# Down projection of the feed-forward taken token chunk by token chunk, with the mixer norm's steps placed inside the last pair

## What is computed

```python
s1, sc1, g1, s2, sc2, g2, s3, sc3, g3 = ada(c, w_ada, b_ada)      # silu(c) @ w_ada + b_ada
h = x + 0.5 * g1 * swiglu(modulate(x, g_ffn1, s1, sc1), w1_gate, w1_up, w1_down)
n = modulate(h, g_mix, s2, sc2)          # rmsnorm(h) * g * (1 + scale) + shift
z = n @ w_in                             # 5192 columns: indexer k, indexer q, q, k, v, conv GLU, gates
...
h = h + g2 * mix
h = h + 0.5 * g3 * swiglu(modulate(h, g_ffn2, s3, sc3), w2_gate, w2_up, w2_down)
```

## Time and profile before

| what | value |
|---|---|
| time, median of 3 runs | 3036.06 us (3033.57 to 3036.47) |
| span of the profiled execution, first to last instruction | 3039.2 us |
| PE busy | 2838.8 us, 93% of the span |
| DVE busy | 1560.0 us, 51% |
| ACT busy | 579.2 us, 19% |
| POOL busy | 748.4 us, 25% |
| mean granted clock of PE | 0.952 |

### The profile page before, as it was taken

The page is one execution under the profiler, slowest core; times in us unless marked ns, Lnnn a source line. Parts: engine busy times, 40 slices in busy tenths (PEclk is TensorE's granted clock), DMA queues, the critical chain, the costliest instruction groups (busy, mean ns, idle before and its releaser), DMA issues.

```text
span 3039.2 us, 43529 instructions
## 1 busy us (share of the span) xinstructions
PE 2838.8 (93%) x16084; PEld 2516.0 (83%) x16084; DVE 1560.0 (51%) x2609; ACT 579.2 (19%) x1056; POOL 748.4 (25%) x419
## 2 busy tenths in 40 slices
PE   7999999999998899999994999888889999999996
PEld 3799999999996667888992356588889999999995
DVE  2443433333347379999998348763243333333335
ACT  1411111111113221122112234420040001010113
POOL 0322222222221236323320000022212332232320
PEclk9999999999999999999996769999989999999998
DMA  6322222222222323211226100123101111111101
GB/s 229 118 70 69 69 69 69 69 69 69 69 66 91 97 57 86 85 35 49 93 81 232 32 1 1 43 87 132 42 22 49 48 41 48 41 48 48 48 21 57
DMA packets 207445, 209.09 MB, mean 69 GB/s; under 512 B 13071, under 2 KB 160643, under 8 KB 206457
## 3 DMA queue, kind: packets, MB, share of 16 engines
q1 hardware_dynamic: 197180, 181.04, 18.9%
q10 hardware_dynamic: 10181, 26.90, 2.7%
HBM read 172.37 MB, written 28.94 MB: 66 GB/s over the span
## 4 chain that ended last, share of the span: by engine, by line
PE 72%; DVE 17%; issue 4%; ACT 3%; DMA 2%; DVEq 1%; SPq 1%; ACTq 0%; POOL 0%; POOLq 0%
PE main L244 19%; PE main L245 18%; PE main L246 18%; DVE top L1129 6%; DVE pick L1142 5%; PE main L1442 3%; PE aux L1469 3%; PE main L1458 2%; PE aux L414 2%; PE main L333 1%; DVE pick L1116 1%; ACT tmp L454 1%; PE aux L344 1%; PE aux L343 1%; PE aux L342 1%
## 5 line engine op out<-in xcount | busy, mean ns | idle before, releaser
L244 PE MATMUL main<-nhi,whi 128*128 128x352 f32 (+1 forms) x3288 | 1076.2, 327 | 29.6 <-DVE nlo L505 18.2
L246 PE MATMUL main<-nhi,wlo 128*128 128x352 f32 (+1 forms) x3288 | 1063.3, 323 | 0.0
L245 PE MATMUL main<-nlo,whi 128*128 128x352 f32 (+1 forms) x3288 | 1062.9, 323 | 0.0
L233 POOL CAST whi<-raw 128x1024 fp32r<-128x1024 f32 x189 | 200.0, 1058 | 2144.3 <-PE main L246 1722.5
L244 PEld LDWEIGHTS main<-nhi,whi 128*128 128x128 f32 (+1 forms) x3288 | 622.5, 189 | 56.4 <-issue 22.8
L245 PEld LDWEIGHTS main<-nlo,whi 128*128 128x128 f32 (+1 forms) x3288 | 624.1, 190 | 0.8
L246 PEld LDWEIGHTS main<-nhi,wlo 128*128 128x128 f32 (+1 forms) x3288 | 622.3, 189 | 0.7
L235 POOL TENSOR_TENSOR wlo<-raw,whi 128x1024 fp32r<-128x1024 f32 x189 | 475.5, 2516 | 15.2
L638 DVE TENSOR_TENSOR tmp<-main,tmp 128x352 f32<-128x352 f32 x132 | 69.2, 524 | 780.0 <-PE main L246 776.1
L659 DVE SCALAR_TENSOR_TENSOR h<-main,ada,h 128x352 f32<-128x352 f32 (+1 forms) x528 | 294.3, 567 | 94.9 <-PE main L246 94.8
L244 PE MATMUL main<-hid_hi,whi 128*128 128x352 f32 x1056 | 341.7, 324 | 0.3
(11 more groups left out here) (224 smaller groups left out, 2570.5 us busy)
## 6 DMA issues: line engine op xcount, KB each, us to landing
ada_raw<-in_w_ada SPq DMA_DIRECT2D x18, 2048.0 KB, 8.7
raw<-in_w_gate SPq DMA_DIRECT2D x44, 512.0 KB, 3.9
raw<-in_w_up SPq DMA_DIRECT2D x44, 512.0 KB, 3.8
raw<-in_w_down SPq DMA_DIRECT2D x44, 512.0 KB, 3.4
raw<-in_w_in SPq DMA_DIRECT2D x40, 512.0 KB, 3.9
gate_d<-zraw ACTq DMA_DIRECT2D x16, 528.0 KB, 2.7
gates<-gate_d SPq DMA_DIRECT2D x16, 528.0 KB, 4.9
zsw<-zraw ACTq DMA_DIRECT2D x50, 132.0 KB, 2.4
```

Source lines behind the costliest of these rows:

```text
L233: pool.tensor_copy(whi[:, slot], raw[:, slot]).then_inc(hi_done, 1)
L244: pe.matmul(bank, whi[:, slot, w], hi(c), start=(i == 0), stop=False)
L245: pe.matmul(bank, whi[:, slot, w], lo(c), start=False, stop=False)
L246: last = pe.matmul(bank, wlo[:, slot, w], hi(c), start=False, stop=(i == n - 1))
```

## The change

1. In every pair of both feed-forwards the down products go chunk by chunk: d = 8 t + 4 half + m. `pe_ada_split` moves from between d = 11 and 12 to ahead of t = 1, between d = 7 and 8. `FFN_ENDS` has 32 in place of 24, since half 0 is now used until d = 19.
2. The last pair of the first feed-forward is taken out of the loops and written out. The mixer norm is a new function, `norm_late`, whose steps stand among those of that pair: squares of chunk 0 on ACT behind d = 7, its sums on PE ahead of d = 12, its reciprocal and scaling on DVE ahead of d = 12 and d = 16, the sums of chunk 1 on PE ahead of d = 20. All squares are made by ACT, into the part of `nlo` that chunk 2 will take (`sq_late`).
3. The remaining steps of the norm are put in another order, and the waits for all 24 updates are gone from PE, ACT and DVE; z's first products wait for their banks instead. `small` gets a place of its own.

```diff
-FFN_ENDS = (5, 6, 9, 12, 24, 36)
+FFN_ENDS = (5, 6, 9, 12, 32, 36)
...
+        sq_late = place("sq_late", [P, KD, TOK], F32, NB + KD * TOK * 4)
...
+            sql = sq_late[:, :, 2 * TC:TOK]
...
+            def square(act, t):
+                done(act, t)
+                if t:
+                    norm_wait(act, q, "mm", t)
+                for half in range(2):
+                    c4 = slice(4 * half, 4 * half + 4)
+                    act.activation(sql[:, c4, :], h[:, c4, tcs(t)], ACT.Square).then_inc(s["sq"], 1)
...
+            def act(act, between):
+                square(act, 0)
+                between()
+                act.wait_ge(mod_set, 4)
+                root(act, 0)
+                square(act, 1)
+                affine(act, 0, (0,))
+                root(act, 1)
+                affine(act, 0, (1,))
+                square(act, 2)
+                affine(act, 1, (0,))
+                root(act, 2)
+                affine(act, 1, (1,))
+                affine(act, 2)
...
+            def rest(dve):
+                low(dve, 0, (0,))
+                rstd_of(dve, 1)
+                low(dve, 0, (1,))
+                done(dve, 1)
+                scale(dve, 1)
+                low(dve, 1, (0,))
+                rstd_of(dve, 2)
+                low(dve, 1, (1,))
+                done(dve, 2)
+                scale(dve, 2)
+                norm_wait(dve, q, "mm", 3)
+                low(dve, 2)
...
-                for half in range(2):
-                    if with_ada and half:
+                for t in range(NTC):
+                    if with_ada and t == 1:
                         if first:
                             pe.wait_ge(c_split, 2)
                         pe_ada_split(pe, INIT_ADA // 4 + j, aux[:, 0])
-                    pe.wait_ge(split_done, T0 + 6 * j + 4 + half + 1)
-                    for t in range(NTC):
+                    for half in range(2):
+                        if t == 0:
+                            pe.wait_ge(split_done, T0 + 6 * j + 4 + half + 1)
                         if half == 0:
                             ffn_wait(pe, q, "hid_lo", 6 * j + 3 + t + 1)
+                        if last and t and half:
+                            if t == 1:
+                                pe_ada_turn(pe, INIT_ADA // 4 + j, aux[:, 1], ada_rows[1])
+                            else:
+                                pe.wait_ge(ada_out, INIT_ADA // 4 + j + 2)
+                            then["pe_sums"](pe, (t - 1,))
                         for m in range(4):
-                            d = 12 * half + 4 * t + m
+                            d = 8 * t + 4 * half + m
...
-                        half, t, m = d // 12, d % 12 // 4, d % 4
-                        c = 4 * half + m
+                        t, c = d // 8, d % 8
+                        if last and d == 12:
+                            dve_ada(dve, INIT_ADA // 4 + j, aux[:, 1])
+                            then["dve_rstd"](dve, 0)
+                        if last and d == 16:
+                            then["dve_scale"](dve, 0)
...
+                if then:
+                    act_step(act, NPAIR - 1)
+                    then["act"](act, lambda: act_ada(act, INIT_ADA // 4 + NPAIR - 1, aux[:, 0], ada_rows[1]))
...
+                if then:
+                    dve_mod(dve, 1, ROW_GM, INIT_ADA // 4 + NPAIR - 1)
+                    dve_mod(dve, 2, ROW_G2, INIT_ADA // 4 + NPAIR - 1)
+                    dve_step(dve, NPAIR - 1, last=True)
+                    dve_half_gate(dve, 2)
+                    then["dve_rest"](dve)
...
         def m1_pe(pe):
-            ffn_wait(pe, "1", "down_free", 24 * NPAIR + 24)
-            norm_m["pe_start"](pe)
             for t in range(NTC):
                 for L in range(2):
                     norm_m["ready"](pe, t)
                     z_product(pe, L, T_Z + L, L % RING, 3 * L, L % 2, 72 if L == 0 else P, ts=(t,))
                     if L == 0 and t == 0:
-                        norm_m["pe_last"](pe)
+                        norm_m["pe_sums"](pe, (2,))
```

More of the change, by code:

```diff
@@ L524, in ffn @@
+        def ffn(q, T0, A0, wg, wu, wd, i, nrm, with_ada, then=None):
+            NLOOP = NPAIR - 1 if then else NPAIR
             f = ffn_sem
@@ L564, in pe_up, with pe_step @@
                         lambda c: nhi[:, c, tcs(t)], lambda c: nlo[:, c, tcs(t)], 0).then_inc(acc_done, 1)
-            def pe_step(pe, j, first):
+            def pe_step(pe, j, first, last=False):
                 for t in range(NTC):
@@ L596, in pe_step @@
                                     m * P, mstride=512).then_inc(acc_done, 1)
-                if with_ada:
+                if with_ada and not last:
                     pe_ada_turn(pe, INIT_ADA // 4 + j, aux[:, 1], ada_rows[1])
@@ L602, in pe @@
                 pe_step(pe, 0, True)
-                with pe.Fori(1, NPAIR) as j:
+                with pe.Fori(1, NLOOP) as j:
                     pe_step(pe, j, False)
+                if then:
+                    pe_step(pe, NPAIR - 1, False, last=True)
             def up_done(j, sub, t, up):
@@ L615, in dve_free, with act_step, chunk_done, dve_step @@
                 dve.drain().then_inc(f["down_free"], 24)
+            def act_step(act, j):
+                for sub in range(2):
+                    for t in range(NTC):
+                        act.wait_ge(acc_done, up_done(j, sub, t, 0))
+                        act.activation(tmp[:, t, :], main[:, t, 0:TC], ACT.Silu).then_inc(f["gate_free"], 1)
+                        ffn_wait(act, q, "up_free", 3 + 6 * j + 3 * sub + t + 1)
+                        act.activation(hid_hi[:, sub, tcs(t)], tmp[:, 3 + t, :], ACT.Copy).then_inc(f["hid_hi"], 1)
+                if with_ada:
+                    for i in range(4):
+                        act_ada_hi(act, INIT_ADA // 4 + j, i)
             def act(act):
                 norm_wait(act, q, "lo", 6)
[L619 to L626, removed]
+                with act.Fori(0, NLOOP) as j:
+                    act_step(act, j)
                     if with_ada:
-                        for i in range(4):
-                            act_ada_hi(act, INIT_ADA // 4 + j, i)
                         act_ada(act, INIT_ADA // 4 + j, aux[:, 0], ada_rows[1])
-            def dve(dve):
-                with dve.Fori(0, NPAIR) as j:
+                if then:
+                    act_step(act, NPAIR - 1)
+                    then["act"](act, lambda: act_ada(act, INIT_ADA // 4 + NPAIR - 1, aux[:, 0], ada_rows[1]))
+            def chunk_done(eng, t):
+                ffn_wait(eng, q, "down_free", 24 * NPAIR + 8 * t + 8)
+            def dve_step(dve, j, last=False):
                     for sub in range(2):
@@ L656, in dve @@
                                               ALU.mult).then_inc(f["samp"], 1)
-                            ffn_wait(dve, q, "samp", 8 * j + 4 * half + m + 1)
+                            ffn_wait(dve, q, "samp", 8 * j + c + 1)
                             dve.tensor_tensor(h[:, c, SEQ:TOK], h[:, c, SEQ:TOK], small[:, c, :], ALU.add)
@@ L661, in dve @@
                             .then_inc(f["down_free"], 1)
-                    if with_ada:
+                    if with_ada and not last:
                         dve_ada(dve, INIT_ADA // 4 + j, aux[:, 1])
+            def dve(dve):
+                with dve.Fori(0, NLOOP) as j:
+                    dve_step(dve, j)
+                if then:
+                    dve_mod(dve, 1, ROW_GM, INIT_ADA // 4 + NPAIR - 1)
[3 more added lines that the diff above has]
+                    then["dve_rest"](dve)
             return {"sp": sp, "pool": pool, "pe": pe, "act": act, "dve": dve, "act_free": act_free,
-                    "dve_free": dve_free}
+                    "dve_free": dve_free, "chunk_done": chunk_done}
         w_in = L0["w_in"]
@@ L854, in z_product @@
             for t in ts:
+                if L < 2:
+                    ffn_wait(pe, "1", "down_free", 24 * NPAIR + 19 + 3 * parity + t)
                 pe.wait_ge(z_free, V + t + 1)
@@ L1921, in _ @@
             act.drain().then_inc(ada_copy, 1)
+            act.drain().then_inc(z_free, 6)
             act_init(act)
```

74 lines of the change are left out of this document (60 added, 14 removed).

## The result

| | changed kernel | kernel before, same chip |
|---|---|---|
| median of 4 runs | 3062.27 us (3059.16 to 3067.95) | 3036.26 us (3033.57 to 3040.64) |
| span of the profiled execution | 3057.2 us | 3039.2 us |

The ratio is 1.0091, with a 95% interval from 1.0072 to 1.0109: the change costs 26.0 us by the medians. The forecast was 3068, with a range from 3049 to 3080.

A forecast was written before the change was run, and what follows sets the result against it. The prediction took PE to bound the feed-forward pairs. Stall +24.2, clock +15 and norm -7 summed to +32 us on a median of 3036.1, giving 3068 us, with a range of 3049 to 3080.

The forecast's parts named there:

- Bound by PE in the pairs: Feed-forward pairs: PE sets the pace, so the change can gain or lose only PE's idle time and clock.
- Stall 11 x 2.2 = +24.2: Conditioning in eleven pairs: PE waits about 2.5 us for `ada_lo` where it waited 0.3, +24.2 us.
- Clock 8 x 1.9 = +15: Behind the conditioning's stall: PE's clock falls in eight of eleven pairs, 1.9 us each, +15 us, bounds 0 and +21.
- The norm -7: Mixer norm in the last pair: chunk 2's z product at about 987 us, before 994.32; -7 us, range -10 to -2.
- clock stays full: Rival, behind the stalls in the pairs: no clock is lost, +15 us in all, 3051 us; chance 0.17.
- Chunk order nothing: Down products in the pairs: apart from the conditioning, the new chunk order costs nothing, 0 us.
- the walk of the last pair: Last pair of the first feed-forward: step-by-step timing of the norm to chunk 2's z product, about 987 us.
- Rotary table 0, bound 2: SP behind the norm: the rotary table goes no sooner than 1004.1 us; cost put at 0, other bound 2 us.
- The sum: Whole kernel: 24.2 + 15 - 7 = +32 us on the median of 3036.1, giving 3068 us.
- What would show it: Profile signs: about 2.5 us idle before L343 in eleven pairs, low PE clock digits from 100 to 950 us, slow conditioning matmuls, late rotary table.

The follow-up runs named there:

- filled kernel: The changed kernel with twelve matmuls of no use ahead of the wait for `ada_lo` in each of eleven pairs; 3050.06 us, ratio 1.0042.
- d = 11 kernel: The changed kernel with the conditioning products moved from ahead of d = 8 to ahead of d = 11; 3025.68 us, ratio 0.996.

## Why the prediction was right, point by point

- **Bound by PE in the pairs: right.** All 32 us of the first ten pairs are PE's own idle time and clock, and filling the idle time alone gave back the clock.
- **Stall 11 x 2.2 = +24.2: right in size**, though one of the eleven stands in the norm's term too (below). There were eleven waits of 2.4 to 2.5 us where 0.3 was. The term was sound because `ada_lo`'s completion could be read as a time after d = 0 (10.1, then 10.2), and nothing upstream of it moved.
- **Clock 8 x 1.9 = +15: right that it is lost, lucky in the count, too high in the price.** Eight pairs lost it, at 1.5 us each, +12. Nothing in the rows gave eight rather than five or eleven, and the kernel with the conditioning moved alone, with the same waits, lost it in five. The 1.9 came from a stretch of other matmuls (fp32 sums), and was a little high even for those: the sums at full clock began at 100.49 and not at 100.65, which makes it 1.8; the conditioning's take 0.63 in place of 0.40, and 3.4 us of them lose 1.5. The rival "clock stays full" was wrong, and the rule beside it lets too much pass: the Trainium skill (TensorE: Matmul & The Clock Gate, Why this matters for your kernels) warns only of idle gaps longer than these, while here 2.4 us of idle time lost the clock in eight pairs of eleven. With the clock full, the change would have come out at about 3050 (3062.27 - 12; the filled kernel measured 3050.06).
- **Chunk order nothing: right**, shown by itself at 1.000.
- **The norm -7: the mechanism right, the sum not.** The step at fault is in the sum: the walk of the last pair already held that pair's stall, and then eleven stalls were added, so that 2.2 us stand twice. By the walk's own measure, last d = 0 to chunk 2's z product, 77.4 us were foreseen and 80.9 came. Of the 3.5 more, 1.5 is the clock of the eleventh conditioning, priced in the other term, so -5.3 stands against -7.3. Another 1.2 came up to the last update, 0.75 of it one L788 held beside POOL's cast (0.94 us in place of 0.19), and 1.7 between that and the first z product, where L390 stood; behind it the steps were 0.9 shorter, although the first z product was slower (6.25 for 5.5). Two guesses inside it came out well: the sums of chunk 1 waited 1.38 (1.4 foreseen), and the table load stood behind the wait for the sums.
- **Rotary table 0, bound 2: 0.9** in the changed kernel, inside the bound. The same idle time was longer by 1.9 in the d = 11 kernel and by 3.6 in the filled one, so the bound was too tight for those.
- **The sum.** +32 was foreseen. By the measured terms, ten stalls of 2.2 outside the last pair, 12 of clock and -5.3, it is 22 + 12 - 5.3 = +28.7; the two profiles show +28.5 up to chunk 2's first z product, and the medians +26.0. The price of the clock and the stall counted twice made the sum too high by 3 and 2.2, the norm's steps ran 2 us longer than in the walk, and so part of the error cancelled. The forecast of 3068 stands 5.7 us above the result.
- **What would show it.** The wait at L343 and the long matmuls were there; the low digits of the clock were not, since a digit is an average over 76 us.

## What to carry to other kernels

Before a step is moved to an earlier place in an engine's program, read for each thing it waits for how long after a common event it is ready, and compare that with the new arrival: here 10.1 us against 7.6, eleven times over, and one call placed three products later turned +26 us into -9. A short wait in front of TensorE can cost more than its length (2.4 us of wait cost 3.9 in eight pairs here), so look for low clock behind it in the timeline, not in the coarse row, and put useful work (here the sums) into the idle time instead of behind it. When one collision between DVE and POOL is taken away, see which DVE step takes its place before counting the gain.

## What was not expected of the hardware

- **Half clock behind 2.4 us of idle time, in some pairs only.** Equal waits of 2.4 to 2.5 us behind some 75 us of full work each lost the clock in 8 of 11 pairs here, and in 5 of 11 in the kernel with the conditioning moved alone. A wait of 1.5 us lost it in none of 11. What decides between equal waits is left open here.
- **A small DVE step held for the whole of a POOL step.** L390, on 72 elements a partition, took 2.06 us beside POOL's subtraction (985.43, 2.35 us long) and 0.19 where POOL was idle; with it moved away, `nlo` took 3.48 there in place of 1.6. The Trainium skill (SBUF — State Buffer, Who interferes with whom) says that a `tensor_scalar` in its two-port form and a `tensor_tensor` with both inputs in SBUF contend with a GpSimd instruction that reads SBUF for a shared pair of ports, which is locked, so that the one that comes second has to stand; the two traces agree, with those numbers. In the changed kernel's timeline, POOL's row:

```profile
985.43 2.35 POOL L236 TENSOR_TENSOR wlo<-raw,whi 128x1024 fp32r<-128x1024 f32 x1
```

and DVE's:

```profile
985.78 2.06 DVE L390 TENSOR_SCALAR ada<-ada 128x72 f32<-128x72 f32 x1
```
